# Both down projections of a gated feed-forward: 14 of 44 weight blocks each computed with seven products instead of eight

## The chip, the core and the metric

The kernel runs on one core of one Trainium2 chip. The metric is device time in microseconds (us). Time before: 2378.66 us, the median of three runs (2378.51 to 2380.51).

## The reference, cut to what matters

The reference is a chain of transformer-like blocks on 256 tokens of width 2048, all float32. The change touches one product in it, the down projection of the gated feed-forward:

```
up = hn @ w_up                                  # (256, 2048) @ (2048, 11264)
gate, val = split(up)                           # 5632 columns each
gate = dwconv_centred(gate, conv_w, conv_b)     # 3 taps over the tokens
ff = (gelu(gate) * val) @ w_down                # (256, 5632) @ (5632, 2048)
h = h + rmsnorm(ff, ffn_norm_post)
```

The width 5632 is worked off in two halves of 2816 = 22 x 128: up projection of half 0, down projection of half 0 ("down0"), up projection of half 1, down projection of half 1 ("down1"). down1 is added to down0, and the sum goes into the rmsnorm.

## The kernel before, in words

**Pieces.** All weights stream through the core once, as 813 pieces ("uses") of at most 128 x 1024 float32 values (512 KB). SP loads a piece into one of four `raw` tiles (L633). ACT copies it into the high half `whi` in the rounded format fp32r (`split`, L1054). DVE forms the low half, `wlo = raw - whi` (L1505). There are six `whi` and six `wlo` tiles. TensorE (PE) then computes each block product from three matmuls: x high by w high, x low by w high, x high by w low (L702). I call these three matmuls, of 512 columns each in the down projections, one product.

**A down projection.** A plain piece of `w_ffn_down` holds 2 x 128 rows (a k-pair) of one block of 512 output columns. There are 11 k-pairs and 4 column blocks, so 44 plain pieces per half. Each is worked on with both token tiles of 128: 2 row tiles x 2 token tiles = 4 products = 12 matmuls. The sums grow in PSUM banks 0 to 3; the banks 4 to 7 are free in these stretches. `natural_out` (L125) writes the order: most of column blocks 0 and 1 one after the other, their last three k-pairs, then blocks 2 and 3. When a column block is complete, its two tiles are evacuated: in down0 by ACT, which copies them to `sn`; in down1 by DVE, which adds them to `sn`. Then ACT squares the result with an accumulated sum (L1101), and DVE multiplies it by the gains of the norm, which lie in X and ev.

**What sets the order.** Each engine runs one loop over all pieces u, in order, and before or after piece u it runs the steps that `layout()` has placed there (`late(u, step)`). At piece u, ACT and DVE split piece u + 5 (AHEAD = 5), and ACT's split of piece i waits until PE has used piece i - 6 (six `whi` tiles). So the two engines run at most five to six pieces ahead of PE. SP loads a piece as soon as DVE's low half of the piece four loads earlier is done. GpSimd (POOL) has no such lookahead: it runs its steps in order and waits for what each needs. A step that waits holds up all that is behind it on its engine.

**Around the change.** In an up projection, each pair of 128 columns takes eight pieces; POOL scales and gates it (four tensor_tensor operations of 128 x 256, L2176), ACT rounds the result to the high half of the x operand and DVE subtracts for the low half (steps `val_high`, `val_low`).

Of the kernel before, what the change touches and what calls it, by code (L numbers as in the profile page):

```python
# [15 lines left out]
T = 256  # L16
D = 2048
# [62 lines left out]
Use = namedtuple("Use", "mat col k0 n cols block first last")  # L80


def layout():
# [41 lines left out]
    def natural_out(kind, operand, mat, ks, last, ahead=None, lag=LAG, lead=2):  # L125
# [15 lines left out]
        return skewed(kind, 3, operand, mat, 1536, ks, ahead, lag, lead)  # L141

# [94 lines left out]
    for half in range(2):  # L237
        for q in range(11):
# [15 lines left out]
            late(e + d + 3, "val_low", f)  # L254
        ends["up", half] = len(uses) - 1
        ends["down", half] = natural_out(f"down{half}", ("ff",), "w_ffn_down", pairs(*range(22 * half, 22 * half + 22, 2)), 3)
    d = ends["down", 1]
    late(d - 40, "load_post", 1)
# [146 lines left out]
def pieces_in_order(x):  # L405
# [8 lines left out]
    for i, s in enumerate(layout()[0]):  # L414
        k = slice(128 * s.k0, 128 * (s.k0 + s.n))
# [7 lines left out]
def block_kernel(nc, a, out):  # L423
# [6 lines left out]
    with ExitStack() as ctx:  # L430
# [6 lines left out]
        hT = sb("hT", [128, KT, T])  # L437
        xa = sb("xa", [128, KT, 2 * T], FR)
# [3 lines left out]
        hn = sb("hn", [128, 2, D])  # L442
        S1 = sb("S1", [128, 16, T])
        S2 = sb("S2", [128, 16, T])
        par = sb("par", [128, NPAR])
        con = sb("con", [128, NCON])
        X = sb("X", [128, 1632])
# [4 lines left out]
        sq = sb("sq", [128, 2, T])  # L452
        ev = sb("ev", [128, 6, T])
# [116 lines left out]
        def post_row(c):  # L570
# [24 lines left out]
        by_act = {b.tile + j for b in {s.block for s in uses} if b.kind in ("ple", "pgate", "down0", "fv", "rv", "rgate") for j in range(b.tiles)}  # L595
# [4 lines left out]
        def pieces(i):  # L600
            s = uses[i]
            r, hi, lo_ = [t[i % m][:, 0:s.n * s.cols] for t, m in ((raw, NRAW), (whi, NHL), (wlo, NHL))]
# [5 lines left out]
        def moved(i):  # L608
            return uses[i].n * (uses[i].cols + (T if i < JOINED else 0))
# [13 lines left out]
        def sync_program(sp, q):  # L623
            def load(i):
                if i >= N:
# [3 lines left out]
                if i >= NRAW:  # L629
                    q.wait_ge(*w_low.of(i - NRAW))  # L630
                    if i - NRAW < JOINED:
                        q.wait_ge(*x_low.of("xa", 0, sum(STARTS[i - NRAW]) - 1))
                sp.dma_start(raw[i % NRAW][:, 0:n], src).then_inc(raw_in[i % NRAW], 16)  # L633
# [5 lines left out]
            for u in range(-1, N):  # L639
                if u >= 0:  # L640
                    load(u + 8)
                for step, *k in at[u]:
# [22 lines left out]
                    elif step == "load_post":  # L665
                        r, = k
                        if r == 0:
# [1684 lines left out]
```

## Time and profile before

| | |
|---|---|
| median of three runs | 2378.66 us |
| the profiled execution: device time | 2378.37 us |
| the profiled execution: span, first to last instruction | 2376.6 us |
| PE busy | 2361.9 us (99%) |
| DVE / ACT / POOL busy | 1522.0 / 1195.6 / 266.2 us |
| down0, from 548.53 to 668.24 us | 119.71 us |
| down1, from 913.46 to 1033.14 us | 119.68 us |

Of the device time, 1.8 us lie outside the span. A matmul's duration in the profile includes its pipeline; the pace of PE is read from the starts of successive matmuls. DVE and ACT are busy about half of the time: they wait for each other and for PE in a regular pattern.

### The profile page before, as it was taken

How to read it: one execution, taken by the hardware profiler on the slowest of the kernel's cores; microseconds unless marked ns; L12 is line 12 of the kernel's file. 1: busy time of each engine (PE TensorE's matmuls, PEld its weight loads, DVE VectorE, ACT ScalarE, POOL GpSimd, SP SyncE). 2: the span in 40 equal slices, each digit the busy share in tenths (PEclk: the TensorE clock that was granted, in tenths of full speed). 3: DMA queues.
4: the chain of work that ended last, by engine and by line, in shares of the span. 5: the costliest groups of instructions: out<-in, count | busy, mean ns of one | idle time of the engine just before them, and what ended most of it. 6: DMA issues, size and time to landing. Idle time of an engine off the chain costs nothing.

```text
span 2376.6 us, 29824 instructions
## 1 busy us (share of the span) xinstructions
PE 2361.9 (99%) x11890; PEld 1982.9 (83%) x11890; DVE 1522.0 (64%) x1965; ACT 1195.6 (50%) x1613; POOL 266.2 (11%) x250
## 2 busy tenths in 40 slices
PE   9999999999999999999999999999999999999999
PEld 7878898888888888888788888887888888888887
DVE  7898577675467775575755556657665554656556
ACT  7876454444444444465655555535444444444442
POOL 1262013321013221000000000001000000000000
PEclk9999999999999999999999999999999999999999
DMA  8446656656665666565566565565665666556653
GB/s 297 156 145 198 215 176 195 188 191 192 193 193 187 188 193 207 191 203 175 176 185 205 158 196 162 167 190 164 191 181 180 214 192 197 177 182 182 189 177 125
DMA packets 122940, 444.04 MB, mean 187 GB/s; under 512 B 13744, under 2 KB 15408, under 8 KB 122288
## 3 DMA queue, kind: packets, MB, share of 16 engines
q1 hardware_dynamic: 122800, 442.12, 59.6%
q8 instruction: 94, 1.54, 0.3%
q14 instruction: 46, 0.38, 0.0%
HBM read 439.97 MB, written 2.10 MB: 186 GB/s over the span
## 4 chain that ended last, share of the span: by engine, by line
PE 93%; DVE 4%; ACT 2%; DMA 1%; issue 1%; SPq 0%; DVEq 0%; ACTq 0%
PE bank L702 92%; DVE wlo L1505 1%; DMA raw<-in_w 1%; DVE ev L1508 1%; ACT whi L1054 1%; PE bank L793 0%; DVE hT L1508 0%; DVE hn L1508 0%; PE bank L978 0%; PE bank L1045 0%; DVE xa L1508 0%; ACT hT L1222 0%; PE bank L1000 0%; DMA hT<-in_xT 0%; ACT L1228 0%
## 5 line engine op out<-in xcount | busy, mean ns | idle before, releaser
L1505 DVE TENSOR_TENSOR wlo<-raw,whi 128x1024 fp32r<-128x1024 f32 (+2 forms) x811 | 1012.9, 1252 | 771.2 <-ACT whi L1054 769.2
L1054 ACT ACTIVATE whi<-raw 128x1024 fp32r<-128x1024 f32 (+1 forms) x813 | 854.7, 1054 | 958.9 <-PE bank L702 942.4
L702 PE MATMUL bank<-xa,whi 128*128 128x512 f32 (+1 forms) x2688 | 841.5, 395 | 6.9 <-DVE xa L1508 3.5
L702 PE MATMUL bank<-whi,xa 128*128 128x512 f32 x2048 | 639.4, 393 | 2.2 <-DVE wlo L1505 1.8
L702 PEld LDWEIGHTS bank<-xa,wlo 128*128 128x128 f32 x2656 | 497.5, 188 | 115.0
L702 PE MATMUL bank<-xa,wlo 128*128 128x256 f32 (+1 forms) x2656 | 520.9, 278 | 0.0
L702 PE MATMUL bank<-whi,xb 128*128 128x512 f32 x1536 | 473.8, 390 | 0.0
L702 PEld LDWEIGHTS bank<-whi,xa 128*128 128x128 f32 x2048 | 379.7, 188 | 82.6 <-issue 4.7
L702 PEld LDWEIGHTS bank<-xa,whi 128*128 128x128 f32 x2688 | 411.0, 188 | 16.1 <-issue 6.6
L702 PE MATMUL bank<-wlo,xa 128*128 128x512 f32 x1024 | 399.1, 390 | 0.0
L702 PEld LDWEIGHTS bank<-whi,xb 128*128 128x128 f32 x1536 | 287.3, 188 | 59.3 <-DVE wlo L1505 0.3
L702 PE MATMUL bank<-wlo,xb 128*128 128x512 f32 x768 | 298.9, 389 | 0.0
L702 PEld LDWEIGHTS bank<-wlo,xa 128*128 128x128 f32 x1024 | 192.2, 188 | 41.1
L702 PEld LDWEIGHTS bank<-wlo,xb 128*128 128x128 f32 x768 | 144.1, 188 | 30.3
L2176 POOL TENSOR_TENSOR S<-S,rs 128x256 f32<-128x256 f32 x88 | 103.4, 1198 | 552.7 <-DVE S L1518 439.3
L2176 POOL TENSOR_TENSOR ev<-ev,con 128x256 f32<-128x256 f32 x32 | 40.6, 1288 | 563.4 <-DVE ev L1518 563.4
L2176 POOL TENSOR_TENSOR hn<-hn,hT 128x512 f32<-128x512 f32 x4 | 7.8, 1972 | 725.0 <-DVE xa L1505 724.9
L702 PE MATMUL bank<-whi,xc 128*128 128x512 f32 x224 | 69.1, 390 | 0.0
L1518 DVE TENSOR_REDUCE S<-bank 128x256 f32<-128x512 f32 x88 | 56.4, 681 | 0.9 <-PE bank L702 0.6
L702 PEld LDWEIGHTS bank<-whi,xc 128*128 128x128 f32 x224 | 41.9, 188 | 8.6
L1518 DVE TENSOR_REDUCE ev<-bank 128x256 f32<-128x512 f32 (+1 forms) x66 | 42.5, 683 | 5.7 <-PE bank L702 5.7
L702 PE MATMUL bank<-wlo,xc 128*128 128x512 f32 x112 | 43.6, 389 | 0.0
(244 smaller groups left out, 1264.5 us busy)
## 6 DMA issues: line engine op xcount, KB each, us to landing
raw<-in_w SPq DMA_DIRECT2D x803, 512.0 KB, 3.8
hT<-in_ln_rows SPq DMA_DIRECT2D x2, 2048.0 KB, 8.3
raw<-in_w SPq DMA_DIRECT2D x9, 256.0 KB, 2.8
X<-in_post SPq DMA_DIRECT2D x3, 768.0 KB, 5.5
S<-in_x SPq DMA_DIRECT2D x4, 512.0 KB, 7.8
hT<-in_x SPq DMA_DIRECT2D x1, 2048.0 KB, 8.2
out<-S SPq DMA_DIRECT2D x8, 256.0 KB, 2.5
hT<-in_xT SPq DMA_DIRECT2D x3, 512.0 KB, 6.8
```

The costliest lines, as they stand in the source:

```text
L702: return pe.matmul(o, w, x, start=start, stop=stop, skip_group_check=True)
L1054: act.activation(hi, r, ACT.Copy).then_inc(*w_high(i))
L1505: return dve.tensor_tensor(o, x, y, op)
L1508: return dve.scalar_tensor_tensor(out=o, in0=x, scalar=s, in1=y, op0=op0, op1=op1)
L1518: return dve.tensor_reduce(o, halves(b), AX, ALU.add)
L2176: return pool.tensor_tensor(o, x, y, op)
```

## The change

In 8 cases of down0 and 6 of down1, a "group" takes the place of two plain pieces. A group covers one k-pair (2 x 128 rows), both token tiles and 1024 output columns, that is a 2 x 2 by 2 x 2 block product. Computed plainly it has eight block products; the change uses a scheme with seven (Strassen's, in Winograd's form). It needs sums of weight blocks and sums of x blocks ("mixtures").

A group has four uses and two loads. `upper` (the first 128 rows, 1024 columns loaded, of which 512 are split; 1 product), `lower` (the other 128 rows; 2 products), `pair_sums` (1024 columns of sums, not loaded; 2 products) and `full_sums` (likewise; 2 products). The step `sums` on POOL makes the sums from the two raw tiles, four tensor_tensor operations of 128 x 512; a raw tile of a group is loaded anew only when POOL has read it too. ACT and DVE split the two sum pieces like loaded ones. Three products gather in the PSUM banks 5, 6, 7 and 4 over all groups of a pair of column blocks ("side" banks).

A mixture of a k-pair is made once per half by one POOL operation of 128 x 512 and four of 128 x 128 (`mixed`), then rounded by ACT (`mixed_high`, 128 x 512) and subtracted by DVE (`mixed_low`, 128 x 512). Those of k-pairs 0 to 3 of down0 and 0 and 1 of down1 are made during the up projections, 2 and 3 of down1 during down1, seven and thirteen uses after its last group of column blocks 0 and 1.

At the end of a pair's groups the side banks are folded: one ACT copy (`fold`) and four DVE operations (`fold`, `fold_end`) with one PSUM operand, 128 x 512 each. In down0 they land in `sn`, and DVE, no longer ACT, combines the banks 0 to 3 with them. In down1 they land in a tile over `xa`, POOL adds them to `sn` (`fold_end` on POOL, four operations of 128 x 512, "joined"), and DVE's evacuation waits for that.

The order (`PLANS`): down0, both pairs of column blocks: 2 plain pieces, 4 groups with 2 plain pieces inside each (one after `lower`, one after `full_sums`), 4 plain pieces. down1, blocks 0 and 1: 6 plain, 2 groups with 2 plain inside each, 8 plain. down1, blocks 2 and 3: 1 plain, 4 groups with 2, 2, 2 and 0 plain inside, 7 plain. The gains of the second norm are loaded ten uses earlier into a tile over `xa`.

```diff
+SUMS = ("pair_sums", "full_sums")
+COMBINED = (0, 1, 2, 3)
+EARLY = ((0, 1, 2, 3), (0, 1))
+def plan(combined, lead, between):
+    turns = [(j, p) for j in range(2) for p in range(11) if p not in combined]
+    groups, at = [], lead
+    for p, n in zip(combined, between):
+        groups.append((p, *turns[at:at + n]))
+        at += n
+    return turns[:lead], groups, turns[at:]
+PLANS = ((plan((0, 1, 2, 3), 2, (2, 2, 2, 2)), plan((0, 1, 2, 3), 2, (2, 2, 2, 2))), (plan((0, 1), 6, (2, 2)), plan((0, 1, 2, 3), 1, (2, 2, 2, 0))))
+IN_PAIRS = (0, 1)
...
+    def paired_out(kind, operand, mat, k, *plans, mixes=()):
...
+        for c, (start, groups, end) in zip((0, 2), plans):
+            pair = [begin(kind, c + j, operand, "natural", 512) for j in range(2)]
+            touched = set()
+            def plain(j, p):
+                first, last = j not in touched, j == 1 and (1, p) == end[-1]
+                touched.add(j)
+                use(pair[j], mat, 512 * (c + j), k + 2 * p, 2, first, last)
+            def part(name, row, col, first, last=False):
+                uses.append(Use(mat, 512 * (c + col), row, 1, 1024, pair[0], first, last, name))
+                return len(uses) - 1
+            for piece in start:
+                plain(*piece)
+            for p, *between in groups:
+                first, last, row = p == groups[0][0], p == groups[-1][0], k + 2 * p
+                a = part("upper", row, 0, first)
+                late(max(a - 7, begun + 2) if k else a - 7, "sums", a)
+                part("lower", row + 1, 0, first)
+                for piece in between[:1]:
+                    plain(*piece)
+                part("pair_sums", row, 0, first)
+                d = part("full_sums", row, 0, first, last)
+                for piece in between[1:]:
+                    plain(*piece)
+            late(d + 1, "fold", kind, c, d)
+            late(d + 2, "fold_end", kind, c)
+            late(d + 2, kind, pair[0])
+            for after, p in mixes if c == 0 else ():
+                mix(d + after, 1, p)
+            for piece in end:
+                plain(*piece)
+        return len(uses) - 1
+    def mix(u, half, p):
+        late(u, "mixed", half, p)
+        late(u + 2, "mixed_high", half, p)
+        late(u + 3, "mixed_low", half, p)
...
+            if half in IN_PAIRS and q in EARLY[half]:
+                mix(e + d + 5, half, q)
         ends["up", half] = len(uses) - 1
...
+    late(d - 50, "load_post", 1)
...
+                turn = turn_of[i]
+                if turn >= NRAW:
+                    before = loaded[turn - NRAW]
+                    q.wait_ge(*w_low.of(before))
...
+                    if uses[before].part == "upper":
+                        q.wait_ge(*pool_val.of("sum", before, 2))
+                    elif uses[before].part == "lower":
+                        q.wait_ge(*pool_val.of("sum", before - 1, 4))
+                sp.dma_start(raw[turn % NRAW][:, 0:n], src).then_inc(raw_in[turn % NRAW], 16)
...
+                def product(B, x, c, start, stop=False):
+                    xh, xl = x
+                    mm(B[:, :], xh, hi[:, 512 * c:512 * c + 512], start)
+                    mm(B[:, :], xl, hi[:, 512 * c:512 * c + 512], False)
+                    return mm(B[:, :], xh, lo_[:, 512 * c:512 * c + 512], False, stop)
...
+                q.wait_ge(*w_low.of(u))
+                if s.part == "upper":
+                    m = product(bank[5], tokens(s.k0, 0), 0, side_free(5), s.last)
+                elif s.part == "lower":
+                    product(bank[n % 4], tokens(s.k0, 0), 0, begins(0))
+                    m = product(bank[(n + 2) % 4], mixture(4), 1, begins(2))
+                elif s.part == "pair_sums":
+                    product(bank[6], mixture(1), 0, side_free(6), s.last)
+                    m = product(bank[4], mixture(3), 1, side_free(4), s.last)
+                else:
+                    product(bank[7], mixture(2), 0, side_free(7), s.last)
+                    m = product(bank[(n + 1) % 4], tokens(s.k0 + 1, 1), 1, begins(1), s.last)
+                m.then_inc(*piece_tile.both(*([("tile", n), ("tile", n + 1)] if s.last else []), ("used", u)))
...
+                if uses[i].part == "pair_sums":
+                    q.wait_ge(*pool_val.of("sum", group_of(i), 2))
+                elif uses[i].part == "full_sums":
+                    q.wait_ge(*pool_val.of("sum", group_of(i), 4))
+                else:
+                    q.wait_ge(*landed(i))
...
+                    elif step == "mixed_high":
+                        half, p = k
+                        q.wait_ge(*pool_val.of("mixed", half, p, 4))
...
+                    elif step == "mixed_low":
+                        half, p = k
+                        m = mixed_set(half, p)
+                        q.wait_ge(*x_high.of("mixed", 11 * half + p))
+                        tt(m[:, 1, :], mixed_v, f32(m[:, 0, :]), ALU.subtract).then_inc(*x_low("mixed", 11 * half + p))
+                    elif step == "fold":
+                        kind, c, d = k
+                        x = [[folded(kind, c, t, j) for j in range(2)] for t in range(2)]
+                        q.wait_ge(*act_evac.of("first", kind, c))
+                        tt(x[0][1], bank[7][:, :], x[0][0], ALU.subtract).then_inc(*vec_val("less", kind, c))
+                        q.wait_ge(*vec_val.now())
+                        tt(x[1][0], x[0][1], bank[4][:, :], ALU.add).then_inc(*vec_val("fold", kind, c, 0))
+                    elif step == "fold_end":
+                        kind, c = k
+                        x = [[folded(kind, c, t, j) for j in range(2)] for t in range(2)]
+                        q.wait_ge(*vec_val.of("fold", kind, c, 0))
+                        tt(x[0][1], x[0][1], bank[6][:, :], ALU.add).then_inc(*vec_val("fold", kind, c, 1))
+                        tt(x[1][1], x[1][0], bank[6][:, :], ALU.add).then_inc(*vec_val("folded", kind, c))
...
+                            if 1 in IN_PAIRS:
+                                q.wait_ge(*pool_val.of("joined", "down1", c - c % 2))
                             q.wait_ge(*piece_tile.of("tile", n))
                             tt(x, x, bank[n % 4][:, :], ALU.add).then_inc(*vec_evac("tile", n))
...
+                    elif step == "mixed":
+                        half, p = k
+                        x = xb[:, 2 * p:2 * p + 2, :]
+                        q.wait_ge(*x_low.of("ff", 22 * half + 2 * p))
+                        q.wait_ge(*x_low.of("ff", 22 * half + 2 * p + 1))
+                        if COMBINED.index(p):
+                            q.wait_ge(*x_low.of("mixed", 11 * half + p - 1))
+                        r = mixed_x.rearrange("p (k t) -> p k t", k=2)
+                        tt(r, f32(x[:, :, 0:T]), f32(x[:, :, T:2 * T]), ALU.add).then_inc(*pool_val("mixed", half, p, 0))
...
+                        tt(v[0], upper[:, 128:256], lower[:, 128:256], ALU.subtract).then_inc(*pool_val("mixed", half, p, 1))
+                        tt(v[2], upper[:, 128:256], upper[:, 0:128], ALU.subtract).then_inc(*pool_val("mixed", half, p, 3))
+                        q.wait_ge(*pool_val.of("mixed", half, p, 1))
+                        tt(v[1], upper[:, 0:128], v[0], ALU.subtract).then_inc(*pool_val("mixed", half, p, 2))
+                        q.wait_ge(*pool_val.now())
+                        tt(v[3], lower[:, 0:128], v[1], ALU.subtract).then_inc(*pool_val("mixed", half, p, 4))
+                    elif step == "sums":
+                        a, = k
+                        pair, full = sums[uses[a].block.kind, uses[a].block.arg]
+                        earlier = [i for i, s in enumerate(uses[:a]) if s.part == "full_sums"]
...
+                            q.wait_ge(*w_low.of(earlier[-1]))
...
+                        up, low = [raw[turn_of[i] % NRAW] for i in (a, a + 1)]
+                        q.wait_ge(*landed(a))
+                        tt(pair[:, 0:512], up[:, 0:512], up[:, 512:1024], ALU.add).then_inc(*pool_val("sum", a, 1))
+                        q.wait_ge(*landed(a + 1))
+                        tt(pair[:, 512:1024], up[:, 512:1024], low[:, 512:1024], ALU.add).then_inc(*pool_val("sum", a, 2))
+                        q.wait_ge(*pool_val.of("sum", a, 1))
+                        tt(full[:, 0:512], pair[:, 0:512], low[:, 512:1024], ALU.add).then_inc(*pool_val("sum", a, 3))
+                        q.wait_ge(*pool_val.now())
+                        tt(full[:, 512:1024], full[:, 0:512], low[:, 0:512], ALU.add).then_inc(*pool_val("sum", a, 4))
+                    elif step == "fold_end" and k[0] == "down1":
+                        kind, c = k
+                        for t in range(2):
+                            for j in range(2):
+                                x = sn[:, t, 512 * (c + j):512 * (c + j) + 512]
+                                q.wait_ge(*emptied(tile_of["down0", c + j] + t))
+                                q.wait_ge(*vec_val.of("folded", kind, c))
+                                m = tt(x, x, folded(kind, c, t, j), ALU.subtract if (t, j) == (1, 0) else ALU.add)
+                        m.then_inc(*pool_val("joined", kind, c))
```

## Rows read from the trace of the kernel before

**Rows 1.** The page: busy time of each engine; granted clock; the chain that ended last.
```profile
PE 2361.9 (99%) x11890; PEld 1982.9 (83%) x11890; DVE 1522.0 (64%) x1965; ACT 1195.6 (50%) x1613; POOL 266.2 (11%) x250
...
PEclk9999999999999999999999999999999999999999
...
PE 93%; DVE 4%; ACT 2%; DMA 1%; issue 1%; SPq 0%; DVEq 0%; ACTq 0%
```

**Rows 2.** Waits, longest in total first: who waited for whom, us, times, longest.
```profile
ACT whi L1054 <- PE bank L702: 942.4, 584, 7.1
DVE wlo L1505 <- ACT whi L1054: 769.2, 540, 6.3
```

**Rows 3.** Windows over down0 and down1: busy us and count of each engine.
```profile
548.53:668.24 119.71, 119.71 (x530) 99.11 (x529) 56.24 (x49) 50.99 (x53) 4.87 (x4) 1.00 0.63 193
913.46:1033.14 119.68, 119.68 (x530) 99.10 (x529) 63.87 (x62) 52.32 (x60) 4.85 (x4) 1.00 0.64 202
```

**Rows 4.** Timeline of PE in down0: start us, us from first start to last end.
```profile
560.12 0.61 PE L702 MATMUL bank<-whi,xb 128*128 128x512 f32 x2
560.57 0.39 PE L702 MATMUL bank<-wlo,xb 128*128 128x512 f32 x1
560.80 0.61 PE L702 MATMUL bank<-whi,xb 128*128 128x512 f32 x2
```

**Rows 5.** Timeline of POOL, later in the kernel, single operations of 128 x 512.
```profile
1644.22 1.30 POOL L2176 TENSOR_TENSOR hn<-hn,hT 128x512 f32<-128x512 f32 x1 [724.86 <-DVE xa L1505]
1645.60 2.15 POOL L2176 TENSOR_TENSOR hn<-hn,hT 128x512 f32<-128x512 f32 x1
1647.72 2.28 POOL L2176 TENSOR_TENSOR hn<-hn,hT 128x512 f32<-128x512 f32 x1
```

**Rows 6.** Timeline of DVE in the same stretch, beside POOL and just after it.
```profile
1644.34 2.26 DVE L1505 TENSOR_TENSOR wlo<-raw,whi 128x1024 fp32r<-128x1024 f32 x1 [0.26 <-ACT whi L1054]
1646.53 2.31 DVE L1505 TENSOR_TENSOR wlo<-raw,whi 128x1024 fp32r<-128x1024 f32 x1
1648.76 2.31 DVE L1505 TENSOR_TENSOR wlo<-raw,whi 128x1024 fp32r<-128x1024 f32 x1
1653.23 1.21 DVE L1505 TENSOR_TENSOR wlo<-raw,whi 128x1024 fp32r<-128x1024 f32 x1
```

**Rows 7.** Line L2176: durations in ns, min/median/max, of one POOL operation.
```profile
L2176 POOL TENSOR_TENSOR S<-S,rs x88: 728/745/1735, 329.1 to 915.2; 128x256 f32<-128x256 f32 x88
L2176 POOL TENSOR_TENSOR hn<-hn,hT x4: 1304/2154/2276, 1644.2 to 1650.1; 128x512 f32<-128x512 f32 x4
```

**Rows 8.** Timeline of DVE in down1, around the evacuation of column block 2.
```profile
1001.86 1.23 DVE L1505 TENSOR_TENSOR wlo<-raw,whi 128x1024 fp32r<-128x1024 f32 x1 [1.50 <-ACT whi L1054]
1003.00 1.27 DVE L1505 TENSOR_TENSOR S<-S,bank 128x512 f32<-128x512 f32 x2
1004.47 1.31 DVE L1505 TENSOR_TENSOR S<-S,X 128x512 f32<-128x512 f32 x2 [0.19 <-ACT ev L1101]
```

**Rows 9.** Timeline of ACT in the same stretch.
```profile
1000.77 1.06 ACT L1054 ACTIVATE whi<-raw 128x1024 fp32r<-128x1024 f32 x1 [1.66 <-PE bank L702]
1003.72 0.63 ACT L1101 ACTIVATE ev<-S 128x512 f32<-128x512 f32 x1 [1.89 <-DVE S L1505]
1004.34 0.62 ACT L1101 ACTIVATE ev<-S 128x512 f32<-128x512 f32 x1
1004.96 1.04 ACT L1054 ACTIVATE whi<-raw 128x1024 fp32r<-128x1024 f32 x1
```

**Rows 10.** The page, DMA issues: count, KB each, median us from issue to landing.
```profile
raw<-in_w SPq DMA_DIRECT2D x803, 512.0 KB, 3.8
```

**Rows 11.** Lines of down0, by form: ACT's evacuation of a bank.
```profile
L1281 ACT ACTIVATE S<-bank 128x512 f32<-128x512 f32 x7 | 4.2, 598 | 3.9 <-PE bank L702 3.7
```

More of the change, by code:

```diff
@@ L79 @@
 Block = namedtuple("Block", "kind arg operand form cols tile tiles")
-Use = namedtuple("Use", "mat col k0 n cols block first last")
+Use = namedtuple("Use", "mat col k0 n cols block first last part", defaults=("",))
+SUMS = ("pair_sums", "full_sums")
[10 more added lines that the diff above has]
+IN_PAIRS = (0, 1)
 def layout():
@@ L414, in pieces_in_order @@
     for i, s in enumerate(layout()[0]):
+        if s.part in SUMS:
+            continue
         k = slice(128 * s.k0, 128 * (s.k0 + s.n))
@@ L594, in block_kernel, with mixed_set, sum_piece, folded @@
         start_of = {s.block: u for u, s in reversed(list(enumerate(uses)))}
-        by_act = {b.tile + j for b in {s.block for s in uses} if b.kind in ("ple", "pgate", "down0", "fv", "rv", "rgate") for j in range(b.tiles)}
+        by_act = {b.tile + j for b in {s.block for s in uses} if b.kind in ("ple", "pgate", "fv", "rv", "rgate") + (() if 0 in IN_PAIRS else ("down0",)) for j in range(b.tiles)}
+        LAST_SUMS = max([i for i, s in enumerate(uses) if s.part in SUMS and s.block.kind == "down0"], default=-1)
+        loaded = [i for i, s in enumerate(uses) if s.part not in SUMS]
+        turn_of = {i: n for n, i in enumerate(loaded)}
+        sums = {("down0", 0): (sn[:, 0, 0:1024], sn[:, 1, 0:1024]), ("down0", 2): (s2[:, 1312:2336], s2[:, 2336:3360]),
+                ("down1", 0): (wide[:, 0:1024], wide[:, 1024:2048]), ("down1", 2): (wide[:, 0:1024], wide[:, 1024:2048])}
+        mixed_x, mixed_v = flat(sq[:, :, :]), s2[:, 3584:4096]
+        xa_flat = flat(xa[:, :, :])
+        def mixed_set(half, p):
+            i = COMBINED.index(p)
+            if half == 0 and i < 2:
+                x = xs1[:, D * i + 1024:D * i + 2048]
+            elif half and i > 1:
+                x = xa_flat[:, 1024 * i + 4096:1024 * i + 5120]
+            else:
+                x = (xs_x, xs_ev)[i % 2][:, :]
+            return x.rearrange("p (a c) -> p a c", a=2)
+        def sum_piece(i):
+            return sums[uses[i].block.kind, uses[i].block.arg][SUMS.index(uses[i].part)]
+        def folded(kind, c, t, j):
+            if kind == "down1":
+                return wide[:, 2048 + 1024 * t + 512 * j:2560 + 1024 * t + 512 * j]
+            return sn[:, t, 512 * (c + j):512 * (c + j) + 512]
+        def group_of(i):
+            while uses[i].part != "upper":
+                i -= 1
+            return i
+        def landed(i):
+            return raw_in[turn_of[i] % NRAW], 16 * (turn_of[i] // NRAW + 1)
         def emptied(n):
@@ L601, in pieces @@
             s = uses[i]
-            r, hi, lo_ = [t[i % m][:, 0:s.n * s.cols] for t, m in ((raw, NRAW), (whi, NHL), (wlo, NHL))]
+            w = 512 if s.part == "upper" else s.n * s.cols
+            r = (sum_piece(i) if s.part in SUMS else raw[turn_of[i] % NRAW])[:, 0:w]
+            hi, lo_ = whi[i % NHL][:, 0:w], wlo[i % NHL][:, 0:w]
             if s.block.form == "stacked":
@@ L608, in moved @@
         def moved(i):
-            return uses[i].n * (uses[i].cols + (T if i < JOINED else 0))
+            return 0 if uses[i].part in SUMS else uses[i].n * (uses[i].cols + (T if i < JOINED else 0))
         def x_tile(j):
@@ L624, in load @@
             def load(i):
-                if i >= N:
+                if i >= N or uses[i].part in SUMS:
                     return
@@ L730, in piece @@
                         start, stop = s.first and k == 0, s.last and k == s.n - 1
+                        if b.form == "natural":
+                            start = n not in begun
+                            begun.add(n)
                         if start and n >= 4:
```

117 lines of the change are left out of this document (102 added, 15 removed).

## The prediction

> **What bounds the kernel now.** I read the page first: PE is busy 99% of the span at the full granted clock, and the chain that ended last is 93% PE [rows 1]. Then the waits: ACT waits for PE, and DVE for ACT [rows 2]; both sit behind the six `whi` tiles and have time to spare. The windows say the same of the two stretches that the change touches: PE 119.7 of 119.7 us, DVE 56 and 64, ACT 51 and 52, POOL 5 [rows 3]. The timeline gives the pace: a product of three matmuls starts every 0.68 us (560.12, 560.80) [rows 4], a plain piece takes 4 x 0.68 = 2.72, and 44 x 2.72 = 119.7 us. So a matmul left out is time won, as long as `wlo` of every piece is there when PE comes to it.
>
> **What is removed.** A group has 7 products for 8: 14 x 0.68 = **9.52 us** off PE. A group takes 4.76 us, with its two plain pieces 10.2. The loads stay at 1 MB per group.
>
> **What is added to DVE and POOL.** A low half of 1024 columns takes DVE 1.21 us, 1.14 from start to start (1001.86 to 1003.00) [rows 8]. POOL's 128 x 512 takes 1.30 us alone. But side by side both stretch: POOL 2.15 and 2.28 us [rows 5], DVE 2.26 to 2.31, with DVE's starts 2.19 and 2.23 us apart, and 1.21 again once POOL is done [rows 6]. They take turns; one pair costs 2.24 us, of which DVE's part is 1.14 and POOL's 1.10. This is what the Trainium skill states (SBUF — State Buffer, section "SBUF: two separate sides"): DVE with two SBUF inputs and GpSimd reading SBUF share a port pair by an exclusive lock, and the loser is fully blocked; the trace agrees (2.24 us a pair). By that page DVE's operations with a PSUM operand stay out of it. With this lock the sum is the one below, without it the first rival's.
>
> Per group with two plain pieces: 5.5 low halves x 1.14 = 6.3 us, four POOL sums x 1.10 = 4.4, together 10.7 us in which the two exclude each other, against 10.2 us of PE.
>
> **down0: no wait.** POOL's loop per group runs from `wlo` of `full_sums` (only then may it overwrite the sums) over four sums and ACT's split back to `wlo`: at most 4 x 2.24 + 1.06 + 1.21 = 11.2 us [rows 5, 6, 9]; from below 4 x 1.30 + 2.3 = 7.5. The first `wlo` of `full_sums` in a pair of column blocks is held only by the `whi` tiles: ACT may split it 2.72 us before the group begins, so it is done near its start, 0.3 in, and PE needs it 6.12 in (0.68 + 1.36 + 2.72 + 1.36). Four loops lose at most 4 x 1.0 = 4.0 of these 5.8 us. The plain pieces between the pairs give it back. The fold and DVE's evacuation, 8 operations of 0.64 us per pair (two took 1.27 [rows 8]), lie in those six plain pieces (16.3 us of PE, 6.8 of low halves); ACT is rid of four copies of 0.60 [rows 11]. down0 gains its full 8 x 0.68 = 5.44 us.
>
> **The early mixtures: nothing.** Six times POOL 3.4 us, ACT 0.6, DVE 0.6, in an up projection where a pair takes 22.3 us ((913.46 - 668.24) / 11, the two windows' edges [rows 3]). The gains' earlier load is 1 MB at a DMA share of 0.64 [rows 3]. If that cover failed, it would show as a delayed split, at most 6 x 0.6 = 3.6 us.
>
> **down1, column blocks 0 and 1: no wait.** Two groups behind six plain pieces, by the same loop.
>
> **down1, column blocks 2 and 3: here it goes wrong.** Let zero be the moment when PE has done the plain piece inside the last group of blocks 0 and 1. Nine plain pieces follow (P1 to P9, 24.5 us), then groups A, B, C, D.
> - ACT and DVE split P6 until 2.35. DVE's `fold_end`, two operations: 3.7. DVE then stands at the evacuation, which waits for POOL's four joins, alone at about 1.27 each: 8.8. ACT stands at the squares behind it.
> - From the evacuation's start to ACT's next split it took 1.96 us (1003.00 to 1004.96 [rows 8, 9]). So P7 is split by ACT until 11.9, and its `wlo` is there at 13.15. PE does not notice: it needs P7 at 16.3.
> - But the raw tile of P7 is the one into which the `lower` of A is loaded. The load lands 3.8 us later [rows 10], at 17.0. SP's later loads queue behind it. POOL's second sum of A waits for it: sum 2 is done at 18.3, sums 3 and 4, in turns with DVE, at 22.7.
> - Mixture 2 stands behind them on POOL: one operation in turns, 24.9; four of 128 x 128. No row shows that size. From 0.73 us at 256 columns and 1.30 at 512 [rows 7] I take 0.44 and 0.08 between two, 2.1 us; bounds: 0.2 and 0.73 each. Done: 27.0.
> - ACT has stood at `mixed_high` since about 20, with everything behind it. 27.55; then two squares at 0.62: 28.8; then `full_sums` of A: 29.85, `wlo` 31.1. PE needs it at 24.5 + 6.1 = 30.6: 0.5 late.
> - Only now may POOL sum for B. `mixed_low` 0.6; four sums and the low halves between them (4 x 1.10 + 1.14 + 0.57 + 1.14): 38.95; another low half, mixture 3 (1.10), `pair_sums` (1.14): 42.3; the four small ones: 44.4; `mixed_high`, split, low half: **47.25** for `full_sums` of B. PE would be there at 40.8. Lost so far: 6.45.
> - C: what stands behind, one low half at a time in turns with POOL, comes 1.5, 0.5 and 0.9 late (after 1.36 us of PE, DVE has `mixed_low`, a POOL turn and a low half to do, 2.84; and so on): 2.9.
> - D has no plain pieces inside. Its sums start at 58.6, take 4 x 1.10 and four low halves (3 x 1.14 + 0.57) = 8.4, then 2.3: 69.3. PE needs it at 67.9: 1.4.
>
> Together 10.75 us of waits against 4.08 gained in down1.
>
> **The sum**, on the profiled execution's own 2378.37 us (0.3 under the median): 2378.37 - 9.52 + 10.75 = **2379.6 us**. What PE waits is of the size of what it saves.
>
> **The rivals.**
> 1. *The chain holds* (faster). If POOL's operations cost 1.30 us beside DVE (the lower bound, POOL alone), then A's sums end at 20.9, mixture 2 at 24.3, `full_sums` of A has its `wlo` at 28.4, B's at 39.9, both in time: 2378.37 - 9.52 = 2368.9 us. Against it stand rows 5 and 6. Half way (the load for A lands earlier, or the small operations take 0.2): the two mixtures give back 2 us, the load's 7 us of idle POOL up to 4; the waits fall to about 5, 2373.9 us.
> 2. *POOL's turn costs more than I take* (slower). If each POOL operation holds DVE for its whole 1.30 us, not 1.10, the loop becomes 4 x 2.44 + 2.3 = 12.0. From 10.2 + 5.8 / 4 = 11.65 on it uses up the lead in down0 too: 4 x 1.8 - 5.8 = 1.4 a pair, 2.8 for both, and in down1 17 operations x 0.2 = 3.4 more: 2379.6 + 6.2 = 2385.8 us. For it: one POOL start follows the other after 2.35 us in rows 5. Against it: DVE's starts, at 2.19 and 2.23. Small operations at 0.73 us add 2 x 1.2 = 2.3 to the forecast, 2381.9, which alone is still no change.
> 3. *The change does not do what it says*: the seven products need as many matmuls as eight. The code has 3 matmuls per product and 7 products; I give it nothing.
>
> **How the numbers follow.** 0.2% (4.8 us) is about what a measurement can tell from no change. Forecast, waits of 5 to 15 us: 0.47, its own range 2374 to 2383.5. Rival 1 with its half-way cases: 0.35, since the loss hangs on one chain of a dozen steps whose start (31.1 against 30.6) is a near thing, and every step that is shorter than I take shortens all behind it. Rival 2: 0.18. Range 2368.5 to 2386.5 us.
>
> **What would show it.** Right: PE waits in down1 only, none above 0.3 us in down0 (114.3 us long instead of 119.7); in down1 the waits begin about 31 us after the last group of blocks 0 and 1, the longest of them, near 3 us, for `wlo` of `full_sums` of B; ACT stands at `mixed_high` some 7 us before; POOL's 128 x 512 shows about 2.2 us beside DVE. down1 is about 126 us long. Wrong: `full_sums` of A ready well before PE (then rival 1 and down1 at 115.6 us), or waits in down0 (rival 2). If POOL's idle time before the second sum of A is missing, my step of the raw tile is wrong.

## The result: slower by 0.44%

The changed kernel takes 2389.7 us (median of 5 runs, 2388.64 to 2391.21) against 2379.15 us for the kernel before (5 runs, 2378.51 to 2380.51): a ratio of 1.0044 with an interval of 1.0033 to 1.0056. The forecast was 2379.6 us within 2368.5 to 2386.5. The time lies 3.2 us above that range, on the side that had a chance of 0.18. The profiled execution took 2389.7 us, its span is 2387.9 us: 11.3 us over the span of before.

The page of the changed kernel, for [rows 1]:

```profile
PE 2359.1 (99%) x11848; PEld 1976.0 (83%) x11848; DVE 1619.6 (68%) x2025; ACT 1216.5 (51%) x1645; POOL 416.5 (17%) x354
...
PEclk9999999999999999999999999999999999999999
...
PE 91%; DVE 5%; ACT 2%; DMA 1%; POOL 1%; issue 1%; SPq 0%; ACTq 0%; DVEq 0%; POOLq 0%
```

PE has 42 matmuls fewer (14 products of 3) and the span is longer all the same. The loss is too small for the slices of the page; it has to be looked for by stretch. Windows of the changed kernel, for [rows 3]: down0; then from down1's first matmul to the first transpose of the next norm, a mark that both kernels have; the same stretch in two parts, down1 itself and what lies behind it; then two short windows in the second part. The columns are start and end, length, busy us and count of PE, PEld, DVE, ACT and POOL, granted clock, DMA share, GB/s.

```profile
549.02:663.80 114.78, 114.78 (x506) 94.62 (x505) 104.26 (x80) 61.06 (x65) 55.48 (x32) 1.00 0.63 202
909.02:1049.84 140.82, 127.07 (x537) 101.04 (x536) 104.50 (x95) 66.48 (x86) 67.21 (x46) 0.98 0.54 176
909.02:1035.66 126.64, 118.63 (x512) 94.84 (x510) 92.36 (x77) 55.53 (x70) 67.21 (x46) 1.00 0.54 175
1035.66:1049.84 14.18, 8.44 (x26) 6.20 (x26) 12.14 (x19) 10.95 (x18) 0.00 (x0) 0.76 0.54 185
1038.00:1044.60 6.60, 3.02 (x13) 2.20 (x13) 5.32 (x6) 4.19 (x6) 0.00 (x0) 0.89 0.82 294
1044.60:1049.80 5.20, 5.20 (x12) 3.97 (x13) 4.69 (x11) 4.38 (x10) 0.00 (x0) 0.50 0.43 132
```

down0 went from 119.71 to 114.78 us, 4.9 won. The second stretch was 125.13 us before (913.46 to 1038.59) and is 140.82: 15.7 lost, where 4.1 were to be won and the forecast lost 6.7. With 0.5 us by which down0 began later (549.02 for 548.53) that is 0.5 - 4.9 + 15.7 = 11.3 us, the whole difference of the spans.

The stretch holds more than down1. Behind down1's 510 matmuls lie 24 of the next product (`p @ w_ple`, two pieces of 12 matmuls), and then the transposes. The kernel before spends 5.45 us on these two pieces:

```profile
1033.14:1038.59 5.45, 5.45 (x25) 4.46 (x24) 4.94 (x12) 4.25 (x11) 0.00 (x0) 1.00 0.35 111
```

So down1 itself went from 119.68 to 126.64 us, 7.0 lost, close to the "about 126 us" of the forecast. The two pieces behind it went from 5.45 to 14.18 us, 8.7 lost, and of them the forecast said nothing. "The end" in what follows means these two pieces. Timeline of PE in the stretch, the lines that begin with a wait (in brackets the idle time and who ended it), and those around the last two:

```profile
977.25 0.74 PE L828 MATMUL bank<-whi,xs_x 128*128 128x512 f32 x2 [0.40 <-DVE wlo L1716]
980.09 0.73 PE L828 MATMUL bank<-whi,xb 128*128 128x512 f32 x2 [1.19 <-DVE wlo L1716]
...
993.05 0.73 PE L828 MATMUL bank<-whi,xs_ev 128*128 128x512 f32 x2 [2.41 <-DVE wlo L1716]
995.89 0.73 PE L828 MATMUL bank<-whi,xc 128*128 128x512 f32 x2 [1.20 <-DVE wlo L1716]
...
1015.12 0.73 PE L828 MATMUL bank<-whi,xa 128*128 128x512 f32 x2 [1.19 <-DVE wlo L1716]
...
1035.43 0.39 PE L828 MATMUL bank<-wlo,xc 128*128 128x512 f32 x1
1037.98 0.73 PE L828 MATMUL bank<-whi,xc 128*128 128x512 f32 x2 [2.16 <-DVE wlo L1716]
...
1044.58 1.19 PE L828 MATMUL bank<-whi,xc 128*128 128x512 f32 x2 [3.58 <-DVE S L1716]
1045.57 0.63 PE L828 MATMUL bank<-wlo,xc 128*128 128x512 f32 x1
1045.99 1.05 PE L828 MATMUL bank<-whi,xc 128*128 128x512 f32 x2
```

Nine waits lie in groups A to D. Counted as what a start comes later than 0.227 us after the one before, they are 0.57, 1.36, 0.40, 0.75, 2.58, 1.36, 0.40, 0.74 and 1.35 us, together 9.5; the forecast had 10.75. The matmul at 1035.43 is the last of down1. The two waits at 1037.98 and 1044.58 (2.3 and 3.7 us by the same count) stand in front of the first and the second piece of the next product, and the forecast had nothing there. After the second one the granted clock is 0.50, the level of 1.2 GHz: a product takes 1.28 us (1045.99 to 1047.28) and not 0.68, twelve matmuls at 0.427 for 0.227 us, 2.4 us in all. So the end costs 2.3 + 3.7 + 2.4 = 8.4 us. To be accounted for are 15.7 lost and 4.1 that were to be won, 19.8 us. The waits of the groups (9.5) and the end (8.4) leave 1.9: 1.0 in the starts right behind the nine waits, and about 0.9 over the stretch.

What the other engines do there. POOL, for [rows 5 and 7], first the sums and the mixture before A, then the second join:

```profile
950.19 5.01 POOL L2422 TENSOR_TENSOR S<-S,wide 128x512 f32<-128x512 f32 x4 [18.42 <-DVE wide L1716]
...
963.18 1.30 POOL L2422 TENSOR_TENSOR wide<-raw 128x512 f32<-128x512 f32 x1 [6.72 <-DMA raw<-in_w]
964.43 4.51 POOL L2422 TENSOR_TENSOR wide<-wide,raw 128x512 f32<-128x512 f32 x2
968.91 2.27 POOL L2422 TENSOR_TENSOR sq<-xb 128x512 f32<-128x512 f32 x1
971.26 0.88 POOL L2422 TENSOR_TENSOR S<-sq 128x128 f32<-128x128 f32 x2
972.10 1.00 POOL L2422 TENSOR_TENSOR S<-sq,S 128x128 f32<-128x128 f32 x2
...
1028.54 5.03 POOL L2422 TENSOR_TENSOR S<-S,wide 128x512 f32<-128x512 f32 x4 [15.83 <-DVE wide L1716]
```

DVE, for [rows 6 and 8]:

```profile
955.30 1.28 DVE L1716 TENSOR_TENSOR S<-S,bank 128x512 f32<-128x512 f32 x2 [5.18 <-issue]
...
967.73 2.31 DVE L1716 TENSOR_TENSOR wlo<-wide,whi 128x1024 fp32r<-128x1024 f32 x1
969.96 1.27 DVE L1716 TENSOR_TENSOR S<-S,bank 128x512 f32<-128x512 f32 x2
...
1033.66 1.29 DVE L1716 TENSOR_TENSOR S<-S,bank 128x512 f32<-128x512 f32 x2 [5.20 <-issue]
...
1036.70 4.63 DVE L1716 TENSOR_TENSOR wlo<-raw,whi 128x1024 fp32r<-128x1024 f32 x4 [0.25 <-ACT whi L1243]
1042.61 1.23 DVE L1716 TENSOR_TENSOR wlo<-raw,whi 128x1024 fp32r<-128x1024 f32 x1 [1.28 <-ACT whi L1243]
1043.75 1.28 DVE L1716 TENSOR_TENSOR S<-S,bank 128x512 f32<-128x512 f32 x2
```

ACT, for [rows 9]:

```profile
973.13 0.63 ACT L1474 ACTIVATE xa<-S 128x512 fp32r<-128x512 f32 x1 [6.38 <-POOL S L2422]
...
974.89 1.04 ACT L1243 ACTIVATE whi<-wide 128x1024 fp32r<-128x1024 f32 x1
...
1034.38 0.63 ACT L1291 ACTIVATE wide<-S 128x512 f32<-128x512 f32 x1 [9.40 <-DVE S L1716]
...
1035.63 3.88 ACT L1243 ACTIVATE whi<-raw 128x1024 fp32r<-128x1024 f32 x4
1041.52 1.06 ACT L1243 ACTIVATE whi<-raw 128x1024 fp32r<-128x1024 f32 x1 [2.01 <-DMA raw<-in_w]
```

Read the end downwards. DVE has done `fold_end` at 1028.5 and stands at the evacuation of block 2 (idle 5.20, put down to "issue": it waits for POOL's join, 1028.54 to 1033.57). ACT stands at the squares behind it (idle 9.40) and splits nothing. When it may go on it has four splits in a row to do (1035.63, 3.88 us), and DVE, right behind it, the four low halves (1036.70): PE, which is through with down1, waits 2.16 for the low half of the next product's first piece. The raw tiles came free late for the same reason: SP issues one load at 1027.3 us and the next at 1037.95. A load behind that gap lands late, and ACT waits 2.01 for it, until 1041.52. And DVE's evacuation of down1's last block (1043.75) stands in DVE's queue behind the low half of that piece (1042.61). PE, whose second piece of the next product needs the banks of that block, waits for it 3.58. One stop of 5 us has come back twice.

The join itself was late too. POOL began it 11.9 us after PE had done D (1016.61 to 1028.54), and the first join 6.9 us after the last group of blocks 0 and 1 (943.27 to 950.19). Between D and the join ACT waited 2.2 and 1.6 us for loads.

### The profile page after: what moved, and what is told of

Read it like the earlier page. It is cut to its first block, busy times and chain, and to the rows that moved or that the text cites. A ratio compares the mean times of both kernels' runs of the same rounds, so it can differ in the third digit from the quotient of the medians.

```text
span 2387.9 us, 30007 instructions
## 1 busy us (share of the span) xinstructions
PE 2359.1 (99%) x11848; PEld 1976.0 (83%) x11848; DVE 1619.6 (68%) x2025; ACT 1216.5 (51%) x1645; POOL 416.5 (17%) x354
## 4 chain that ended last, share of the span: by engine, by line
PE 91%; DVE 5%; ACT 2%; DMA 1%; POOL 1%; issue 1%; SPq 0%; ACTq 0%; DVEq 0%; POOLq 0%
PE bank L828 89%; DVE wlo L1716 2%; DMA raw<-in_w 1%; ACT whi L1243 1%; DVE ev L1719 1%; POOL wide L2422 1%; PE bank L977 0%; DVE hT L1719 0%; DVE hn L1719 0%; PE bank L1229 0%; PE bank L1162 0%; DVE xa L1719 0%; ACT hT L1412 0%; DMA hT<-in_xT 0%; PE bank L1184 0%
## 5 line engine op out<-in xcount | busy, mean ns | idle before, releaser
L1716 DVE TENSOR_TENSOR wlo<-raw,whi 128x1024 fp32r<-128x1024 f32 (+2 forms) x811 | 1041.9, 1293 | 660.3 <-ACT whi L1243 658.3
L1243 ACT ACTIVATE whi<-raw 128x1024 fp32r<-128x1024 f32 (+2 forms) x813 | 844.6, 1046 | 871.6 <-PE bank L828 828.6
L828 PE MATMUL bank<-whi,xb 128*128 128x512 f32 x1396 | 431.2, 390 | 2.3 <-DVE wlo L1716 2.3
L828 PEld LDWEIGHTS bank<-whi,xb 128*128 128x128 f32 x1396 | 260.7, 188 | 58.0 <-DVE wlo L1716 4.3
L828 PE MATMUL bank<-wlo,xb 128*128 128x512 f32 x698 | 271.8, 389 | 0.0
L828 PEld LDWEIGHTS bank<-wlo,xb 128*128 128x128 f32 x698 | 131.0, 188 | 27.5
```

Source lines behind the costliest of these rows:

```text
L828: return pe.matmul(o, w, x, start=start, stop=stop, skip_group_check=True)
L1243: act.activation(hi, r, ACT.Copy).then_inc(*w_high(i))
L1716: return dve.tensor_tensor(o, x, y, op)
```

## The experiments

All times are medians; the kernel before took 2378.64 us beside the first four, 2378.94 beside the next four and 2379.54 beside the last two. "The stretch" is always from down1's first matmul to the first transpose of the next norm, with the two pieces behind down1 in it: 125.13 us before, 140.82 changed.

**Only down0's groups.**

```diff
-IN_PAIRS = (0, 1)
+IN_PAIRS = (0,)
-    late(d - 50, "load_post", 1)
+    late(d - 40, "load_post", 1)
```

> The change in down0 alone; down1 is the plain one of before. Theory A (the groups pay where DVE and ACT are not held up by the join and the late mixtures; all of the loss lies in down1): down0 lasts 114.8 us and down1 119.7, total 4.9 us under before, about 2374.2 us. Theory B (the groups cost about what they save wherever they stand, because DVE and POOL exclude each other): about 2379, with PE waiting for wlo in down0.

Measured: 2373.81 us, ratio 0.998 [0.9971, 0.999]. Its windows, down0 and the stretch:

```profile
548.42:663.21 114.79, 114.79 (x507) 94.63 (x506) 104.04 (x80) 61.07 (x65) 55.78 (x32) 1.00 0.62 203
908.42:1033.56 125.14, 125.14 (x555) 103.59 (x553) 68.83 (x73) 56.58 (x70) 4.85 (x4) 1.00 0.64 198
```

down0 alone makes the kernel faster, by 4.8 us of its 5.44. DVE goes from 56 to 104 us busy there, POOL from 5 to 56, and PE waits nowhere. All of the loss comes with down1's groups.

**The evacuation three uses later in down1.** DVE and ACT then have splits to do while POOL joins.

```diff
-            late(d + 2, kind, pair[0])
+            late(d + (5 if k else 2), kind, pair[0])
```

> The changed kernel, but in down1 the evacuation of the first column block of each pair (and the squares and gains that follow it) stands three pieces later, at d + 5 for d + 2. Theory A (DVE stands waiting for POOL's join; that delays the raw tile of P7, with it the sums of A and all behind, and at the end of down1 the evacuation of the last block): the waits for groups A to C go, and so do the 8.4 us at the end of down1; at most 2 us remain at D: about 2389.7 - 9 - 8.4 = 2372 us. Theory B (the exclusion of DVE and POOL makes the waits; where DVE waits matters little): the waits of 10.3 us at A to D stay; 2381 us if the end of down1 is mended all the same, 2389 if not.

**Mixtures 2 and 3 earlier.** Their steps move from 24 and 30 uses into down1 to its start: POOL's part stands 3 and 10 uses in, so no longer between the sums of the groups A to D. ACT's and DVE's parts follow POOL's by 4 to 6 uses, no longer 2 and 3.

```diff
-                mix(d + after, 1, p)
+                u = begun + {2: 3, 3: 10}[p]
+                late(u, "mixed", 1, p)
+                late(u + (5 if p == 2 else 4), "mixed_high", 1, p)
+                late(u + (6 if p == 2 else 5), "mixed_low", 1, p)
```

> The changed kernel, but mixtures 2 and 3 of down1 are made at the start of down1 (POOL steps 3 and 10 uses into it, ACT's part 4 to 5 uses later), so that neither POOL nor ACT has them between the groups A to D. Theory A: full_sums of A has its wlo about 6 us earlier and B's chain is 5 us shorter, the waits at A to C (about 8.5 us) go; the waits at D (1.4) and at the end of down1 (8.4) stay: about 2381 us. Theory B: the sums themselves are too slow beside DVE, A to D still wait 5 us or more: 2386 or above. If the mixtures only moved their cost, waits appear at the groups of blocks 0 and 1.

**Both edits.**

> Both edits together: evacuation three pieces later and mixtures 2 and 3 at the start of down1. Theory A: the 14 groups pay in full but for up to 2 us at D: down0 114.8, down1 116 to 118, total about 2371 us. Theory B: no better than the change in down0 alone, 2374 or above.

Measured: evacuation later 2384.2 us, ratio 1.0022 [1.0012, 1.0032], stretch 135.35; mixtures earlier 2383.9, 1.0021 [1.0012, 1.003], stretch 134.98; both 2379.17, 1.0002 [0.9993, 1.0011], stretch 129.52. Set against its own runs of before, each wins 5.0 to 5.3 us on the changed kernel and the two together 10.0 (10.5 - 5.6, 10.5 - 5.3, 10.5 - 0.5), so they add up: each takes something of its own out of the in-order queues. The second takes out two things at once, POOL's work between the groups and ACT's wait for it, and no run parts them. PE's remaining waits in the stretch, with the evacuation later (the longest in the groups and the longest at the end):

```profile
989.92 0.73 PE L828 MATMUL bank<-whi,xs_ev 128*128 128x512 f32 x2 [2.36 <-DVE wlo L1716]
...
1035.24 0.70 PE L828 MATMUL bank<-whi,xc 128*128 128x512 f32 x2 [2.52 <-DVE S L1716]
```

with the mixtures earlier (the longest in D and the last; one of 0.97 stands in front of the end's first piece):

```profile
1009.33 1.06 PE L831 MATMUL bank<-whi,xa 128*128 128x512 f32 x2 [1.84 <-DVE wlo L1719]
...
1039.25 0.70 PE L831 MATMUL bank<-whi,xc 128*128 128x512 f32 x2 [3.62 <-DVE S L1719]
```

and with both (besides these three, one of 0.32 in D and one of 0.43 at the transposes):

```profile
1008.86 0.73 PE L831 MATMUL bank<-whi,xa 128*128 128x512 f32 x2 [1.83 <-DVE wlo L1719]
...
1031.06 0.70 PE L831 MATMUL bank<-whi,xc 128*128 128x512 f32 x2 [1.49 <-DVE S L1719]
...
1036.38 0.70 PE L831 MATMUL bank<-whi,xc 128*128 128x512 f32 x2 [2.35 <-DVE S L1719]
```

The later evacuation takes away the waits in A, the earlier mixtures those of A to C but for one of 1.27 us and one of 0.09. For the later evacuation and for both I had expected some 2372 and 2371 us; they came out 12 and 8 us above. With the later evacuation alone I had the waits of A to C and the 8.4 us at the end go: those of B and C stayed, and at the end 5.8 us did (starts 2.7, 1.1 and 0.6 late, 1.4 at the lower clock). With both, D keeps 2.5 us and the end 4.8. The mixtures alone were expected at 2381 and came out 3 us above. So neither edit, nor both, mends the end.

**The sums in blocks 2 and 3 only 16 columns wide.**

```diff
+                        if uses[a].block.kind == "down1" and uses[a].block.arg == 2:
+                            n = 16
+                        else:
+                            n = 512
-                        tt(pair[:, 0:512], up[:, 0:512], up[:, 512:1024], ALU.add).then_inc(*pool_val("sum", a, 1))
+                        tt(pair[:, 0:n], up[:, 0:n], up[:, 512:512 + n], ALU.add).then_inc(*pool_val("sum", a, 1))
...
```

> The changed kernel, but in column blocks 2 and 3 of down1 POOL's four sums of a group cover 16 columns each instead of 512 (work left out: the sums are mostly missing), so that POOL is quick there and hardly excludes DVE. All waits, joins and mixtures stay. Theory A (the waits at A to D are the length of the chain sums, mixture, ACT, DVE; the exclusion adds to it): the chain is 6 to 8 us shorter per group, no wait at A to D (10.3 us less), and as D's sums are there early, ACT and the raw tiles are not held up after D and most of the 8.4 us at the end goes: 2372 to 2375 us. Theory C (the sums hardly matter, it is DVE standing at the join and ACT at the mixture): waits at B stay at 3 us or more, 2382 or above.

This kernel leaves most of the sums out. Measured: 2374.24 us, ratio 0.9979 [0.997, 0.9988], stretch 124.11, as expected. No wait is left in A to D, and at the end a single one (and 0.43 at the transposes):

```profile
1030.71 0.70 PE L828 MATMUL bank<-whi,xc 128*128 128x512 f32 x2 [1.67 <-DVE S L1716]
```

With the order of work untouched, the sums' time is what makes A to D wait. It is not enough alone for A to C: with the mixtures earlier and the sums whole, most of those waits went too, so they come from the chain of both. This run shortens POOL's operations and takes away DVE's turns with them at once, so it doesn't part the two. The sums are worth 15.2 us of the changed kernel's time (10.5 + 4.7), for they feed the end too: here the join begins 7.6 us after D (1007.12 to 1014.69), not 11.9. It still takes 5.0 us, and DVE still stands for 5.19.

**Plain pieces inside D, as in A to C** (5 pieces behind it for 7).

```diff
-plan((0, 1, 2, 3), 1, (2, 2, 2, 0))
+plan((0, 1, 2, 3), 1, (2, 2, 2, 2))
```

> The changed kernel, but the last group D of down1 has two plain pieces inside like the others (five plain pieces after it instead of seven). Theory A (after D the four raw tiles are held until POOL's fourth sum, ACT stands at full_sums of D in front of all plain pieces, the loads then come in a burst and land late, so fold, join and evacuation start some 5 us late): the wait at D (1.4) goes and the 8.4 us at the end shrink to 3 or less; A to C keep their 8.5: about 2383 us. Rival (five pieces after D are too few for a join of 5 us and the two evacuations; it is the number of pieces that counts): the waits at the end stay or grow, 2389 or above.

Measured: 2386.45 us, ratio 1.003 [1.0018, 1.0043], stretch 138.06. I had expected 2383 us, or 2389 and above if the number of pieces behind D was what counted; it came out between. D's wait is gone, and the end holds one longer wait:

```profile
1042.85 1.19 PE L828 MATMUL bank<-whi,xc 128*128 128x512 f32 x2 [4.61 <-DVE S L1716]
```

It costs 4.8 us, one in front of the first piece 0.3, and the twelve matmuls at the lower clock 2.4 as before: 7.5 for 8.4. So pieces inside D do not mend the end. They are taken from behind D, though, where the join has its room, and this run can't tell how much of the end the one gave and the other took. The clock also fell in B, for some 3.5 us behind a wait of 2.37.

**The joins 16 columns wide.**

```diff
-                                m = tt(x, x, folded(kind, c, t, j), ALU.subtract if (t, j) == (1, 0) else ALU.add)
+                                m = tt(x[:, 0:16], x[:, 0:16], folded(kind, c, t, j)[:, 0:16], ALU.subtract if (t, j) == (1, 0) else ALU.add)
```

> The changed kernel, but POOL's four joins at the end of each pair of down1 cover 16 columns each instead of 512 (work left out: most of the folded side sums never reach the output). DVE then stands about 1 us, not 5, before the evacuation. Theory A (the join delays P7's raw tile and with it A, and at the end of down1 the load behind which the last evacuation stands): sums 3 and 4 of A end some 3 us earlier, A to C lose at most 6 us of their 8.9, and the wait of 3.6 us and the half clock at the end go; what is left there (2 us or so) is the late start after D. About 2389.7 - 4 - 6 = 2380 us. Rival (it is D's lateness that makes the end wait, the join adds little): the waits at the end stay above 5 us, 2385 or above.

This kernel leaves most of the joins out. Measured: 2381.23 us, ratio 1.0007 [0.9998, 1.0016], stretch 132.50; expected some 2380. The waits in A are gone, most of those in B to D stay, and at the end the pair of 2.16 and 3.58 has become one:

```profile
1038.72 0.97 PE L828 MATMUL bank<-whi,xc 128*128 128x512 f32 x2 [2.54 <-DVE S L1716]
```

So the join's 5 us is a cause of the end, but not the only one: 2.7 us and 1.6 us in matmuls at the lower clock are left without it, 4.3 of 8.4. The join begins 12.8 us after D here (1014.25 to 1027.01): D's lateness is untouched.

**Without D, with both edits of order** (13 groups: 8, 2 and 3; the second pair has 2 plain pieces, three groups with 2 each, 8 plain).

```diff
-plan((0, 1, 2, 3), 1, (2, 2, 2, 0))
+plan((0, 1, 2), 2, (2, 2, 2))
-mixes=((7, 2), (13, 3)) if half else ()
+mixes=((7, 2),) if half else ()
```

> Both edits of e4, and group D of down1 (with mixture 3) left to plain pieces: 2 plain, 3 groups with 2 plain inside, 8 plain. 13 groups. Theory A (what e4 still waits comes from D, which has no plain pieces inside): no wait of 0.5 us left in down1; 13 x 0.68 = 8.8 us under before: 2370 to 2371 us. Rival (the join beside DVE, 8 us long, makes the end wait by itself): 3 us or more stay at the end, 2373 or above.

Measured: **2371.15 us** (2370.52 to 2372.45), ratio 0.9966 [0.9953, 0.9979], where 2370 to 2371 us was expected. This beats both kernels: 7.8 us under the one before. Its stretch, one window:

```profile
910.35:1032.61 122.26, 122.26 (x539) 100.78 (x538) 102.89 (x92) 65.34 (x83) 61.17 (x37) 1.00 0.63 202
```

PE waits nowhere: 125.13 less five products of 0.68 would be 121.7. The second join here, on POOL, and the two evacuations of DVE around it:

```profile
1010.14 7.93 POOL L2425 TENSOR_TENSOR S<-S,wide 128x512 f32<-128x512 f32 x4 [15.40 <-DVE wide L1719]
```

```profile
1018.16 1.29 DVE L1719 TENSOR_TENSOR S<-S,bank 128x512 f32<-128x512 f32 x2 [1.24 <-POOL S L2425]
...
1026.94 1.28 DVE L1719 TENSOR_TENSOR S<-S,bank 128x512 f32<-128x512 f32 x2
```

The join takes 7.93 us for 5.03, as DVE splits beside it, and yet costs PE nothing: DVE stands at the evacuation for 1.24 us, not 5.20. It begins 7.5 us after the last group (1002.68 to 1010.14), not 11.9 as with D.

**The same with the evacuation where the change has it.**

```diff
-            late(d + (5 if k else 2), kind, pair[0])
+            late(d + 2, kind, pair[0])
```

> As e7 (13 groups, mixture 2 early), but the evacuation of the first column block of each pair stays where the change has it, at d + 2. If the later evacuation is needed: the block of 5 us by the join makes A late by up to 1 us and the end of down1 wait 2 us: 2373 to 2375. If eight plain pieces after C and no mixture between the groups are enough: 2371, like e7.

Measured: 2375.01 us, ratio 0.9981 [0.9971, 0.999], stretch 124.56, where 2373 to 2375 us was expected if the later evacuation is needed. One wait stands at the end (and 0.45 at the transposes):

```profile
1032.01 0.70 PE L831 MATMUL bank<-whi,xc 128*128 128x512 f32 x2 [1.43 <-DVE S L1719]
```

The place of the evacuation alone is worth 3.3 us (7.8 won, and 4.5 here, each against its own runs of before), 2.3 of them in the stretch.

**Three groups in each pair of column blocks of down1, with both edits** (14 groups, as many as the change).

```diff
-plan((0, 1), 6, (2, 2)), plan((0, 1, 2, 3), 1, (2, 2, 2, 0))
+plan((0, 1, 2), 4, (2, 2, 2)), plan((0, 1, 2), 2, (2, 2, 2))
```

> As e7, but three groups in either pair of down1 (4 plain, 3 groups with 2 plain inside, 6 plain; then 2, 3 groups, 8), 14 groups in all. Theory A: the whole 9.5 us: 2369 to 2370 us, if six plain pieces after the first pair's groups are enough for the join. If not, PE waits at the groups of blocks 2 and 3 again, 1 to 4 us: 2371 to 2374.

Measured: 2377.95 us, ratio 0.9995 [0.9985, 1.0004], stretch 128.29, against 2369 to 2374 expected: a miss. Two of its six waits of note:

```profile
943.69 0.74 PE L831 MATMUL bank<-whi,xb 128*128 128x512 f32 x2 [0.57 <-DVE wlo L1719]
969.79 0.71 PE L831 MATMUL bank<-whi,xb 128*128 128x512 f32 x2 [1.32 <-DVE S L1719]
```

The product saved is 0.68 us and the group costs 6.8 us (2377.95 for 2371.15). The wait of 0.57 stands in the third group of blocks 0 and 1. The one of 1.32 stands in front of the first piece of blocks 2 and 3, which needs the banks of block 0: POOL joins until 968.87, and DVE evacuates them only at 968.96. Six plain pieces lie between the pairs' groups here for eight, and the first join does not fit.

## Why the prediction was wrong, step by step

- **"down0: no wait"** was right: no wait above 0.3 us, 114.78 us for 114.3. The missing 0.5 us is in the pace: of 504 starts, some 70 come 0.231 to 0.241 us after the one before and not 0.226 to 0.227. The only-down0 kernel shows it too (4.8 us won for 5.44).
- **POOL's turn** was right: sums 3 and 4 of down1's groups take a median of 2.15 us, as the operations in [rows 5] do, and DVE's low half 2.31 (967.73). The Trainium skill (SBUF — State Buffer, section "Who interferes with whom") says that a DVE instruction with at most one SBUF input, outside the two-port modes, does not contend with GpSimd; the operations with a bank have one SBUF input. The trace agrees: POOL's operation at 968.91 ends 1.1 us after DVE's low half does (971.18 for 970.04), and DVE's pair with the bank beside it (969.96) takes 1.27 us, as without POOL.
- **"down1, column blocks 2 and 3"**, the chain up to D, was right in order and size. The plain piece inside the last group of blocks 0 and 1 ends at 946.2, the zero. From there, forecast and measured: evacuation 8.8 and 9.1, the load for A's `lower` 17.0 and 16.9, mixture 2 done 27.0 and 26.9, `full_sums` of A 31.1 and 31.0, of B 47.25 and 46.85, D 69.3 and 68.9. POOL's idle time before A's second sum (6.72) and ACT's before `mixed_high` (6.38) are there. The size of POOL's 128 x 128, chosen between 0.2 and 0.73, is 0.46 us with DVE at rest (beside a low half 1.32 to 1.46). The waits came to 9.5 us, and 1.0 behind them: 10.5 for 10.75. down1 is 126.6 us long, as the forecast said (about 126).
- **The step that failed is the end of that sum.** It stopped at D: "Together 10.75 us of waits". The change has a second join, 12 us behind D, and I gave it no line, though I had priced the first one at 5 us of standing DVE and ACT. The first one had nine plain pieces before the next late thing, and PE did not notice. The second one had seven in all, began 11.9 us into their 19, and right behind them came the evacuation of the last block and the splits of the next product. What the sum put at nothing is therefore the path behind down1: the two pieces of the next product took 14.18 us for 5.45. Of that, 2.3 + 3.7 us were waits and 2.4 were lost in matmuls at half the clock: 8.4.
- **The sum mended**: forecast 2379.6, less 0.25 (waits of the groups that were shorter), plus 8.4 (the end), 0.5 (pace in down0), 0.9 (pace in the stretch), 0.5 (what lies before down0) gives 2389.65; measured 2389.7.
- **Rival 2** (POOL's turn dearer) had a time near the range's edge, and is not what happened: down0 has no waits.
- **Rival 1's half-way cases** did not come either, though its premise was sound: take steps out of the chain (either edit, or short sums), and most of the waits in A to C go.

What stays open: how much of the 8.4 us comes from D's lateness and how much from the join. Short joins, with D as late as before, leave 4.3 us of it (2.7 of wait, 1.6 at the lower clock). Short sums, with the whole join but D on time, leave 1.8, and 0.6 at the transposes. No run had both. Nor did any run take away the lower clock by itself.

## What to carry to other kernels

Where engines take their work in order, follow a chain across them past the end of the stage, into the product behind it, and price each instance of a step anew: the second join met less slack than the first. Put work that does not depend on a helper engine's result in front of the wait for it: an evacuation three uses later, and two mixtures made twenty uses earlier, won 5 us each without one operation less. Price the last piece of a saving by itself: the fourteenth group saves 0.68 us of PE and made the kernel 6.8 us slower in blocks 0 and 1 (2377.95 for 2371.15) and 8.3 us as D (2379.17 us, each set against its own runs of before).

## What the runs showed of the hardware

- The granted clock fell to 0.50 in PE's wait of 3.58 us and stayed there for 5.2 us behind it; likewise with 4.61 us (plain pieces inside D). Behind 2.16 us (at 1037.98) and behind 2.41 us (at 993.05) it stayed at 1.00. One wait's length alone does not decide: with the mixtures earlier it was 0.54 over 2.8 us behind a wait of 1.84, with plain pieces inside D 0.59 over 4.2 us (994.0 to 998.2) behind one of 2.37, with short joins 0.56 over 3.4 us (991.6 to 995.0) behind one of 1.95, with both edits 1.00 behind one of 2.35.
- Loads of 512 KB that are issued one close behind the other land later: those of 1016.2, 1017.4, 1018.5 and 1019.6 us took 3.6, 5.1, 5.2 and 5.3 us to land, those of 1024.8 and 1027.3 us 3.7 and 3.6. The page's median hardly moved (3.9 us, for 3.8 in [rows 10]), but this is the line of landing times of the eleven from 1016.2 to 1041.4 us in the changed kernel, the first of which go out 1.1 us apart:

```profile
DMA to landing us min/median/max: 3.5/4.0/5.3
```

- Four POOL operations of 128 x 512 take 5.0 us with DVE at rest and 7.9 us beside its low halves: less than four turns of 2.24, or 9.0. In the kernel without D only three low halves lie beside them (1009.98, 1012.20 and 1014.92): 5.0 + 3 x 1.14 would be 8.4, and the join took 7.93; the first low half had begun before it.
